# Conditioning visits of a fused decoder layer regrouped from eight to five, and three more of its first projections' phases taken in quarters

## The chip, the cores and the metric

One core of a Trainium2 chip runs the whole kernel. The metric is the device time of one execution in microseconds (us). Times of the profile are counted from the first instruction of the profiled execution.

## The reference, cut to what matters

One layer of a hybrid decoder for 256 prompt tokens and 8 sample tokens (264 columns), D = 2048, all in float32:

```python
mod = silu(c) @ ada_w + ada_b                      # 9 conditioning vectors
shift, scale, gate = split(mod, 3)
h = rmsnorm(x, g_pre) * (1 + scale) + shift
z = h @ w_in                                       # a_x, a_g, q, k, v, b_g
y_a = pool_mixer(a_x) * silu(a_g)
y_b = groupnorm(retention(q, k, v)) * silu(b_g)
ya, yb = y_a @ w_a_proj, y_b @ w_b_proj
g_a, g_b = split(sigmoid(h @ w_merge + b_merge), 2)
out = rmsnorm((g_a * ya + g_b * yb) @ w_out, g_post)
y = x + gate * out
```

## The kernel before, in words

The kernel is written engine by engine, each with its own program and with semaphores between them; the order in each program is the order of the work. All transfers are issued by SyncE, one after the other. Weights come in units of 1 MB (128 partitions by 2048 numbers, `UNIT`). A product in float32 is made of three passes of the faster format: ScalarE copies a unit to its high part (`w_hi`, `split`, L792), VectorE subtracts it from the raw unit (`w_lo`, L1132), and TensorE multiplies high by high, high by low and low by high (`sum_up`, L442 to L444), 48 matmuls of 264 columns for a unit, one project of some 5.8 us.

**The first phases (L589 to L611).** h can't be made before the conditioning is known, so the kernel goes over K in eight phases p, each for two of the 16 tiles of h. Phase p needs four units of conditioning weights (`ada_phase`, 64 small matmuls, L416), a selection (`select`, L435), the making of two tiles of h on VectorE and ScalarE (`make_h`, `split_h`, `low_h`), and then the products of slices 2p and 2p+1 (`first_w`): each slice holds, for these two tiles of K, eight of the 16 first gate projections. Five of the 16 sums stay in banks of PSUM (`own`); eleven pass through two banks in turn (`pass_through`) and are added up in SBUF by VectorE (`take_sum`, L1165), so that TensorE waits for VectorE two sums later. Slices 0 to 6 are handled in quarters (`BY_QUARTER`, L70): VectorE reports every quarter of the low part, TensorE takes two of the eight units of a slice per quarter (`quarter`, L529), and an even slice begins with a special order (`first_quarter`, L545). In this form (p = 1 to 3) TensorE's conditioning for phase p stands behind the first quarter of slice 2p-1, and VectorE takes sums of slice 2p-1 ahead of the pieces of slice 2p. From p = 4 on (L605) a slice is waited for as a whole, the conditioning stands ahead of slice 2p-1 (`odd_slice`, `even_slice`), and VectorE splits all four pieces of slice 2p ahead of the first sum of slice 2p-1 (L1268 to L1270). The first slice is loaded by one transfer (`load_slice(0)`, L283).

**The middle.** Stream units 0 to 71: eight heads of retention, four groups of pooling, eight units for ya.

**The last stretch.** Projects q = 0 to 31 (`project(12, q, ...)`, L715) are units 72 to 103: for q = 0 to 7 only yb's projections, since their 16 gates came out of the first phases; they were stored to DRAM and are read back in pairs (`sig_a`, `sig_b`, `load_gates`, L371). `combine(n)` on VectorE (L1482) makes gate times ya plus gate times yb; it needs the output of project n, which ScalarE takes from its bank (L1027). The gates' buffers are single, so the load of pair n waits for combine(n - 1), `mf_ready`. Between projects TensorE makes the gate's part of the conditioning: 16 units (`ada1`), two at each of eight visits behind projects 3, 7, 11, 14, 18, 22, 26 and 29 (`COND_VISITS`, L76, L720), 16 small matmuls a unit as the trace counts them (`gate_unit`, L426), out of a ring of two (`gate_ring`). Their loads stand in SyncE's passes q of this loop:

```python
for i in range(75, 107):
    q = i - 75
    load(12, i - 72)
    if q < FIRST // 2 - 1:
        load_gates(q + 1)
    for s in range(2):
        if q - 1 - s in COND_VISITS[:7]:
            load_cond(COND_VISITS.index(q - 1 - s) + 1, s)
```

`load` waits until VectorE has split the unit that used the slot before (`lo_ready`), `load_gates(q + 1)` for combine(q), `load_cond` until TensorE has used the slot. SyncE stands still at each such wait.

Of the kernel before, what the change touches and what calls it, by code (L numbers as in the profile page):

```python
# [69 lines left out]
BY_QUARTER, HIGH_BY_QUARTER = (0, 1, 2, 3, 4, 5, 6), (0, 1, 2, 4, 6)  # L70
# [5 lines left out]
COND_VISITS = (3, 7, 11, 14, 18, 22, 26, 29)  # L76
# [20 lines left out]
def build(nc, stream, first_w, ada0, ada1, xT, x_tok, consts_in, headc, trig, cnt_in, poolw, spool,  # L97
# [5 lines left out]
    with ctx:  # L103
        def sb(name, shape, dt=f32, stack=ctx):
            return stack.enter_context(nc.sbuf_tensor(name, shape, dt))
# [66 lines left out]
        late = ExitStack()  # L172
        m_hi = sb("m_hi", [128, KT, NT], f32r, late)
        ya_out = sb("ya_out", [128, KT, NT], f32, late)
        m_lo = sb("m_lo", [128, KT, NT], f32r, late)
# [30 lines left out]
        ada_half = sem("ada_half")  # L206
# [29 lines left out]
        gate_loaded = [sem(f"gate_loaded{s}") for s in range(2)]  # L236
# [14 lines left out]
        Y_BANK = [TR, TV, SC, O1, ST, P[0], P[1], TR]  # L251

# [4 lines left out]
        def _(sp):  # L257
# [25 lines left out]
            load_slice(0)  # L283
            for p in range(1, 4):
                load_slice(2 * p - 1)
                load_ada(p, range(4))
                load_slice(2 * p)
            for p in range(4, 8):
                load_ada(p, (0, 1))
                load_slice(2 * p - 1)  # L290
                load_ada(p, (2, 3))
                load_slice(2 * p)
# [84 lines left out]
            def load_cond(v, s):  # L377
                if v >= 1:
                    sp.wait_ge(gate_used, 2 * v - 1 + s)
                sp.dma_start(gate_ring[:, s, :], ada1[2 * v + s]).then_inc(gate_loaded[s], 16)  # L380
# [3 lines left out]
            load_cond(0, 0)  # L384
            load_cond(0, 1)
            for i in range(75, 107):
                q = i - 75
                load(12, i - 72)
                if q < FIRST // 2 - 1:
                    load_gates(q + 1)  # L390
                for s in range(2):
                    if q - 1 - s in COND_VISITS[:7]:
                        load_cond(COND_VISITS.index(q - 1 - s) + 1, s)
# [15 lines left out]
        def _(pe):  # L409
# [183 lines left out]
            for p in range(1, 4):  # L593
# [8 lines left out]
            first_quarter(6)  # L602
            for n in range(1, 4):
                quarter(6, n)
            for p in range(4, 8):  # L605
                ada_phase(p)
                odd_slice(2 * p - 1, between=p)
                if p < 7:
                    even_slice(2 * p)
# [105 lines left out]
            for q in range(32):  # L715
# [4 lines left out]
                if q in COND_VISITS:  # L720
                    v = COND_VISITS.index(q)
                    if v == 4:
                        pe.wait_ge(gpart_ready, 1)
                    for s in range(2):
                        pe.wait_ge(gate_loaded[s], 16 * v + 16)
                        gate_unit(2 * (v % 4) + s, gate_ring[:, s, :]).then_inc(gate_used, 1)
# [54 lines left out]
        def _(act):  # L781
# [74 lines left out]
            for p in range(1, 4):  # L856
# [6 lines left out]
            for p in range(4, 8):  # L863
                split_slice(2 * p)
                ada_copy(p)
                split_h(p)
                split_slice(2 * p + 1)
# [250 lines left out]
        def _(dve):  # L1118
# [115 lines left out]
            for p in range(1, 4):  # L1234
# [23 lines left out]
            for p in range(4, 8):  # L1258
# [419 lines left out]
```

## Time and profile before

| | before |
|---|---|
| median of 3 runs | 929.7 us (929.62 to 929.83) |
| the profiled execution | 929.46 us |
| its span, first to last instruction | 927.6 us |
| TensorE busy | 911.0 us, 98% |
| VectorE busy | 554.2 us, 60% |
| ScalarE busy | 420.3 us, 45% |
| DMA | 234.58 MB, mean 253 GB/s |
| mean granted TensorE clock | 0.997 |
| chain that ended last, by engine | PE 93%, DMA 4%, DVE 1% |

PE is TensorE, PEld its weight loads, DVE VectorE, ACT ScalarE, SP or SPq SyncE, L a line of the kernel. Matmuls overlap: one is listed with 0.28 us, but the next starts 0.12 us after it, so the distances of starts are to be read. An idle time in brackets stands before the instruction of its row, with what ended it. Granted clock is the share of full speed: 1.00 is 2.4 GHz, 0.50 is 1.2 GHz.

### The profile page before, as it was taken

The page shows a single profiled execution, that of the slowest core. Times are in us where ns is not written, and L with a number is a line of the kernel's source. Part 1 is how long each engine was busy: PE and PEld are TensorE (multiplying, and loading weights), DVE is VectorE, ACT ScalarE, POOL GpSimd, SP SyncE. Part 2 cuts the span into 40 slices and gives each one's busy share as a digit, 9 for nine tenths or more (in the row PEclk, how much of TensorE's full clock was granted, in tenths as well). Part 3 has the DMA queues.
Part 4 walks back from the last instruction along what each step waited for, and adds up shares of the span by engine and source line. Part 5 has one row for each costly group of instructions (what it writes and reads, how often), then busy time and mean ns, then how long its engine had stood idle before and what let it go on. Part 6 is the DMA issues. An engine that isn't in the chain of part 4 may idle for free.

```text
span 927.6 us, 18788 instructions
## 1 busy us (share of the span) xinstructions
PE 911.0 (98%) x7816; PEld 873.8 (94%) x7816; DVE 554.2 (60%) x809; ACT 420.3 (45%) x537; POOL 54.9 (6%) x38
## 2 busy tenths in 40 slices
PE   6999999999999999999999999999999999999997
PEld 4888889999999999999999999999999999999997
DVE  4667776467575766757576655336454434446664
ACT  3424237556465665646454433444343434343330
POOL 0000000001102020120202122000000000000000
PEclk9999999999999999999999999999999999999999
DMA  9999985848576584857675555466787676744535
GB/s 365 420 420 418 419 330 198 323 145 318 182 292 231 206 301 152 323 188 275 243 274 177 194 203 188 152 272 189 279 309 289 243 259 241 258 156 177 182 137 187
DMA packets 43467, 234.58 MB, mean 253 GB/s; under 512 B 8848, under 2 KB 14224, under 8 KB 16656
## 3 DMA queue, kind: packets, MB, share of 16 engines
q1 hardware_dynamic: 43408, 233.72, 68.2%
q8 instruction: 46, 0.75, 0.3%
q14 instruction: 13, 0.11, 0.0%
HBM read 219.33 MB, written 14.38 MB: 252 GB/s over the span
## 4 chain that ended last, share of the span: by engine, by line
PE 93%; DMA 4%; DVE 1%; SPq 1%; POOL 1%; issue 0%; ACT 0%; DVEq 0%; POOLq 0%
PE bank L442 25%; PE bank L443 25%; PE bank L444 25%; DMA raw<-first_w 4%; PE bank L507 3%; PE bank L508 3%; PE bank L509 3%; PE bank L416 2%; PE bank L426 2%; PE bank L657 1%; PE bank L702 1%; PE bank L641 1%; DVE raw L1564 1%; PE bank L552 1%; PE bank L642 0%; PE bank L666 0%
## 5 line engine op out<-in xcount | busy, mean ns | idle before, releaser
L442 PE MATMUL bank<-h_hi,w_hi 128*128 128x264 f32 x1280 | 368.2, 288 | 0.0
L443 PE MATMUL bank<-h_lo,w_hi 128*128 128x264 f32 x1280 | 362.8, 283 | 0.0
L444 PE MATMUL bank<-h_hi,w_lo 128*128 128x264 f32 x1280 | 362.5, 283 | 0.0
L1132 DVE TENSOR_TENSOR w_lo<-raw,w_hi 128x2048 fp32r<-128x2048 f32 x119 | 272.3, 2288 | 141.2 <-PE bank L444 139.4
L792 ACT ACTIVATE w_hi<-raw 128x2048 fp32r<-128x2048 f32 x120 | 229.8, 1915 | 40.9 <-DMA raw<-stream 20.9
L442 PEld LDWEIGHTS bank<-h_hi,w_hi 128*128 128x128 f32 x1280 | 241.1, 188 | 6.1 <-issue 5.8
L443 PEld LDWEIGHTS bank<-h_lo,w_hi 128*128 128x128 f32 x1280 | 241.3, 189 | 0.3
L444 PEld LDWEIGHTS bank<-h_hi,w_lo 128*128 128x128 f32 x1280 | 240.1, 188 | 0.0
L442 PE MATMUL bank<-yb_hi,w_hi 128*128 128x264 f32 x256 | 72.8, 284 | 0.0
L507 PE MATMUL bank<-h_hi,w_hi 128*128 128x264 f32 x240 | 71.7, 299 | 1.1 <-DVE gate_sum L1165 0.9
L442 PE MATMUL bank<-m_hi,w_hi 128*128 128x264 f32 x256 | 72.7, 284 | 0.0
L444 PE MATMUL bank<-yb_hi,w_lo 128*128 128x264 f32 x256 | 72.6, 283 | 0.0
L443 PE MATMUL bank<-m_lo,w_hi 128*128 128x264 f32 x256 | 72.5, 283 | 0.0
L444 PE MATMUL bank<-m_hi,w_lo 128*128 128x264 f32 x256 | 72.5, 283 | 0.0
L443 PE MATMUL bank<-yb_lo,w_hi 128*128 128x264 f32 x256 | 72.5, 283 | 0.0
L509 PE MATMUL bank<-h_hi,w_lo 128*128 128x264 f32 x240 | 68.2, 284 | 0.0
L508 PE MATMUL bank<-h_lo,w_hi 128*128 128x264 f32 x240 | 68.2, 284 | 0.0
L507 PEld LDWEIGHTS bank<-h_hi,w_hi 128*128 128x128 f32 x240 | 45.2, 188 | 5.5 <-issue 3.8
L442 PEld LDWEIGHTS bank<-yb_hi,w_hi 128*128 128x128 f32 x256 | 48.2, 188 | 0.8 <-issue 0.8
L1079 POOL TENSOR_TENSOR sq_t<-o_t 128x528 f32<-128x528 f32 x8 | 23.5, 2940 | 425.3 <-DVE o_t L1351 425.3
L443 PEld LDWEIGHTS bank<-m_lo,w_hi 128*128 128x128 f32 x256 | 48.2, 188 | 0.0
L443 PEld LDWEIGHTS bank<-yb_lo,w_hi 128*128 128x128 f32 x256 | 48.2, 188 | 0.0
(189 smaller groups left out, 1205.9 us busy)
## 6 DMA issues: line engine op xcount, KB each, us to landing
raw<-stream SPq DMA_DIRECT2D x120, 1024.0 KB, 5.0
ada_ring<-ada SPq DMA_DIRECT2D x31, 1024.0 KB, 19.4
raw<-first_w SPq DMA_DIRECT2D x16, 1024.0 KB, 16.0
gate_ring<-ada SPq DMA_DIRECT2D x16, 1024.0 KB, 6.9
s_t<-sret SPq DMA_DIRECT2D x8, 1024.0 KB, 5.0
v_all<-v_dram SPq DMA_DIRECT2D x8, 1024.0 KB, 6.7
nret_s<-s_t SPq DMA_DIRECT2D x8, 1024.0 KB, 7.8
x_t<-xT SPq DMA_DIRECT2D x4, 528.0 KB, 6.0
```

The costliest lines, as they stand in the source:

```text
L416: mm = pe.matmul(TR[32 * j:32 * j + 32, 0:AW], cpad[:, 8 * (j % 2) + 2 * s + kk, :], w[:, at:at + AW], start=(s == 0 and kk == 0), stop=(s ...
L426: mm = pe.matmul(TR[32 * j:32 * j + 32, 0:AW], cpad[:, 2 * v + kk, :], w[:, at:at + AW], start=(v == 0 and kk == 0), stop=(v == 7 and kk = ...
L442: pe.matmul(out, wh[:, cols], hi[:, k, :], start=(k == 0), stop=False)
L443: pe.matmul(out, wh[:, cols], lo[:, k, :], start=False, stop=False)
L444: mm = pe.matmul(out, wl[:, cols], hi[:, k, :], start=False, stop=(k == depth - 1))
L507: pe.matmul(out, hi, h_hi[:, k, :], start=(start and t == 0), stop=False)
L508: pe.matmul(out, hi, h_lo[:, k, :], start=False, stop=False)
L509: mm = pe.matmul(out, lo, h_hi[:, k, :], start=False, stop=(stop and t == 1))
L552: pe.matmul(FIRST_BANK[u][:, 0:NT], w[:, w_slot, at:at + 128], h[:, 2 * p + t, :], start=start, stop=False)
L792: act.activation(w_hi[:, c % 3, :], raw[:, c % 3, :], ACT.Copy).then_inc(hi_ready, 1)
L1079: pool.tensor_tensor(sq_t[:, :, :], o_t[:, :, :], o_t[:, :, :], ALU.mult).then_inc(sq_ready, 1)
L1132: dve.tensor_tensor(lo, raw[:, c % 3, :], hi.bitcast(f32), ALU.subtract).then_inc(lo_ready, 1)
```

## The change

Three things, with no matmul and no byte more or less.

- The first slice is loaded in two halves, each with a semaphore of its own; ScalarE waits for the first half ahead of its first quarter and for the second ahead of its third.
- Phases 4 to 6 take the form of phases 1 to 3. `BY_QUARTER` goes up to slice 12, the loops over p on all engines now run `range(1, 7)` in quarters, and only phase 7 keeps the form of before. SyncE asks for slice 2p-1 ahead of all four conditioning units of phase p, not behind the first two.
- The gate's 16 units are used at five visits, behind projects 3, 7, 18, 23 and 28, four, four, three, three and two at a time. Three places of a unit each are added to the ring of two, on memory that is not in use yet (`cond_lo` and `cond_hi` on the second halves of `m_lo` and `m_hi`, `cond_ya` on `ya_out`), and a table says in which pass which unit is loaded.

```diff
-BY_QUARTER, HIGH_BY_QUARTER = (0, 1, 2, 3, 4, 5, 6), (0, 1, 2, 4, 6)
+BY_QUARTER, HIGH_BY_QUARTER = tuple(range(13)), (0, 1, 2, 4, 6, 8, 10, 12)
-COND_VISITS = (3, 7, 11, 14, 18, 22, 26, 29)
+COND_VISITS = {3: (0, 1, 2, 3), 7: (4, 5, 6, 7), 18: (8, 9, 10), 23: (11, 12, 13), 28: (14, 15)}
+COND_PLACE = (0, 1, 2, 3, 0, 1, 2, 3, 0, 1, 4, 0, 1, 4, 0, 1)
+COND_LOADS = {0: 1, 1: 2, 3: 3, 4: 4, 5: 5, 6: 6, 7: 7, 11: 8, 12: 9, 13: 10, 19: 11, 20: 12, 21: 13, 24: 14, 25: 15}
...
+        COND = [gate_ring[:, 0, :], gate_ring[:, 1, :], cond_lo[:, :], cond_hi[:, :], cond_ya[:, :]]
...
-            load_slice(0)
-            for p in range(1, 4):
+            for n in range(2):
+                half = slice(UNIT // 2 * n, UNIT // 2 * n + UNIT // 2)
+                sp.dma_start(raw[:, 2, half], first_w[0][:, half]).then_inc((slice_half, raw_loaded[2])[n], 16)
+            for p in range(1, 7):
                 load_slice(2 * p - 1)
                 load_ada(p, range(4))
                 load_slice(2 * p)
-            for p in range(4, 8):
+            for p in range(7, 8):
...
-            def load_cond(v, s):
-                if v >= 1:
-                    sp.wait_ge(gate_used, 2 * v - 1 + s)
-                sp.dma_start(gate_ring[:, s, :], ada1[2 * v + s]).then_inc(gate_loaded[s], 16)
+            def load_cond(u):
+                place = COND_PLACE[u]
+                if u == 3:
+                    sp.wait_ge(proj_done, 80)
+                elif u == 10:
+                    sp.wait_ge(mf_ready, FIRST // 2)
+                elif place in COND_PLACE[:u]:
+                    last = max(n for n in range(u) if COND_PLACE[n] == place)
+                    sp.wait_ge(gate_used, last + 1)
+                sp.dma_start(COND[place], ada1[u]).then_inc(gate_loaded[place], 16)
...
                 if q < FIRST // 2 - 1:
                     load_gates(q + 1)
-                for s in range(2):
-                    if q - 1 - s in COND_VISITS[:7]:
-                        load_cond(COND_VISITS.index(q - 1 - s) + 1, s)
+                if q in COND_LOADS:
+                    load_cond(COND_LOADS[q])
...
                 if q in COND_VISITS:
-                    v = COND_VISITS.index(q)
-                    if v == 4:
-                        pe.wait_ge(gpart_ready, 1)
-                    for s in range(2):
-                        pe.wait_ge(gate_loaded[s], 16 * v + 16)
-                        gate_unit(2 * (v % 4) + s, gate_ring[:, s, :]).then_inc(gate_used, 1)
+                    for u in COND_VISITS[q]:
+                        if u == 8:
+                            pe.wait_ge(gpart_ready, 1)
+                        pe.wait_ge(gate_loaded[COND_PLACE[u]], 16 * COND_PLACE[:u].count(COND_PLACE[u]) + 16)
+                        gate_unit(u % 8, COND[COND_PLACE[u]]).then_inc(gate_used, 1)
...
             def split_quarter(j, n):
-                if n == 0:
+                if j == 0 and n == 0:
+                    act.wait_ge(slice_half, 16)
+                elif n == 0 or (j == 0 and n == 2):
                     act.wait_ge(raw_loaded[slot], 16 * (j // 3) + 16)
```

**SyncE, passes q = 2 to 4 of the last stretch, and the first row of the next.** raw is a project's weights, sig_a and sig_b are a pair of gates, gate_ring and cond_hi places of conditioning units. Before:

```order
L261 DMA raw<-stream 128x2048 [waits lo_ready]
L374 DMA sig_a<-gates_dram 128x264 [waits mf_ready]
L375 DMA sig_b<-gates_dram 128x264
L261 DMA raw<-stream 128x2048 [waits lo_ready]
L374 DMA sig_a<-gates_dram 128x264 [waits mf_ready]
L375 DMA sig_b<-gates_dram 128x264
L261 DMA raw<-stream 128x2048 [waits lo_ready]
L374 DMA sig_a<-gates_dram 128x264 [waits mf_ready]
L375 DMA sig_b<-gates_dram 128x264
L380 DMA gate_ring<-ada 128x2048 [waits gate_used]
L261 DMA raw<-stream 128x2048 [waits lo_ready]
```

After:

```order
L276 DMA raw<-stream 128x2048 [waits lo_ready]
L391 DMA sig_a<-gates_dram 128x264 [waits mf_ready]
L392 DMA sig_b<-gates_dram 128x264
L276 DMA raw<-stream 128x2048 [waits lo_ready]
L391 DMA sig_a<-gates_dram 128x264 [waits mf_ready]
L392 DMA sig_b<-gates_dram 128x264
L403 DMA cond_hi<-ada 128x2048 [waits proj_done]
L276 DMA raw<-stream 128x2048 [waits lo_ready]
L391 DMA sig_a<-gates_dram 128x264 [waits mf_ready]
L392 DMA sig_b<-gates_dram 128x264
L403 DMA gate_ring<-ada 128x2048 [waits gate_used]
```

A conditioning load has come into pass 3: unit 3, into cond_hi, behind that pass's pair. Before, passes 2 and 3 had none, and the load of pass 4 was unit 2; it is unit 4 now.

**TensorE, the first visit.** Before:

```order
L444 MATMUL bank<-yb_hi,w_lo 128x264
L426 MATMUL bank<-gate_ring,cpad 32x256 [waits gate_loaded0]
L426 MATMUL bank<-gate_ring,cpad 32x256 x7
L426 MATMUL bank<-gate_ring,cpad 32x256 [waits gate_loaded1]
L426 MATMUL bank<-gate_ring,cpad 32x256 x7
L442 MATMUL bank<-yb_hi,w_hi 128x264 [waits taken,lo_ready]
L443 MATMUL bank<-yb_lo,w_hi 128x264
```

After:

```order
L465 MATMUL bank<-yb_hi,w_lo 128x264
L447 MATMUL bank<-gate_ring,cpad 32x256 [waits gate_loaded0]
L447 MATMUL bank<-gate_ring,cpad 32x256 x7
L447 MATMUL bank<-gate_ring,cpad 32x256 [waits gate_loaded1]
L447 MATMUL bank<-gate_ring,cpad 32x256 x7
L447 MATMUL bank<-cond_lo,cpad 32x256 [waits gate_loaded2]
L447 MATMUL bank<-cond_lo,cpad 32x256 x7
L447 MATMUL bank<-cond_hi,cpad 32x256 [waits gate_loaded3]
L447 MATMUL bank<-cond_hi,cpad 32x256 x7
L463 MATMUL bank<-yb_hi,w_hi 128x264 [waits taken,lo_ready]
```

Where two units stood there are now four, and the third and fourth wait for loads of their own.

**VectorE, phase 4.** gate_sum rows are sums, w_lo rows pieces of a slice, mods and v_t the making of h. Before:

```order
L1191 SCALAR_TENSOR_TENSOR x_t<-x_t,consts,rstd 128x264 x2
L1149 TENSOR_TENSOR w_lo<-raw,w_hi 128x512 [waits slice_sums,hi_ready]
L1149 TENSOR_TENSOR w_lo<-raw,w_hi 128x512 x3
L1165 TENSOR_TENSOR gate_sum<-bank,gate_sum 128x264 [waits sums_taken,slice_sums]
L1203 TENSOR_TENSOR mods<-bank,consts 128x36 [waits hf_ready,sel_done]
L1213 TENSOR_TENSOR v_t<-x_t,mods 128x2x8 [waits h_lo_ready,h_hi_ready,xn_ready,mod_ready]
L1210 TENSOR_SCALAR v_t<-x_t,mods 128x256
L1216 TENSOR_TENSOR v_t<-v_t,mods 128x2x8 [waits hf_ready]
L1210 TENSOR_SCALAR v_t<-x_t,mods 128x256
L1165 TENSOR_TENSOR gate_sum<-bank,gate_sum 128x264 [waits sums_taken,slice_sums] x2
```

After:

```order
L1209 SCALAR_TENSOR_TENSOR x_t<-x_t,consts,rstd 128x264 x2
L1183 TENSOR_TENSOR gate_sum<-bank,gate_sum 128x264 [waits sums_taken,slice_sums] x2
L1221 TENSOR_TENSOR mods<-bank,consts 128x36 [waits hf_ready,sel_done]
L1231 TENSOR_TENSOR v_t<-x_t,mods 128x2x8 [waits h_lo_ready,h_hi_ready,xn_ready,mod_ready]
L1228 TENSOR_SCALAR v_t<-x_t,mods 128x256
L1234 TENSOR_TENSOR v_t<-v_t,mods 128x2x8 [waits hf_ready]
L1228 TENSOR_SCALAR v_t<-x_t,mods 128x256
L1183 TENSOR_TENSOR gate_sum<-bank,gate_sum 128x264 [waits sums_taken,slice_sums]
L1167 TENSOR_TENSOR w_lo<-raw,w_hi 128x512 [waits slice_sums,hi_quarter]
L1183 TENSOR_TENSOR gate_sum<-bank,gate_sum 128x264 [waits sums_taken,slice_sums]
```

Before, four pieces of slice 8 stood ahead of the first sum of slice 7 and of `mods`; now two sums and `mods` come first, and one piece follows.

## Rows read from the trace of the kernel before

**Rows 1.** The page: busy time and share of each engine; bytes moved in 40 slices.

```profile
PE 911.0 (98%) x7816; PEld 873.8 (94%) x7816; DVE 554.2 (60%) x809; ACT 420.3 (45%) x537; POOL 54.9 (6%) x38
...
GB/s 365 420 420 418 419 330 198 323 145 318 182 292 231 206 301 152 323 188 275 243 274 177 194 203 188 152 272 189 279 309 289 243 259 241 258 156 177 182 137 187
```

**Rows 2.** Chain that ended last, 6 to 34 us: start us, us, what.

```profile
6.54 16.78 DMA raw<-first_w
23.34 0.63 ACT w_hi L807
...
24.42 1.72 PE bank L552 x12
```

**Rows 3.** Timeline of the weight loads, 32 to 38 us: start us, us, instruction [idle before].

```profile
35.64 0.59 PEld L416 LDWEIGHTS bank<-ada_ring,cpad 128*32 128x32 f32 x16 [0.40 <-DMA ada_ring<-ada]
```

**Rows 4.** Timeline of TensorE: where a phase's conditioning begins, seen in short windows.

```profile
49.56 0.42 PE L416 MATMUL bank<-ada_ring,cpad 128*32 128x256 f32 x4
...
66.15 0.63 PE L416 MATMUL bank<-ada_ring,cpad 128*32 128x256 f32 x7
...
80.78 0.42 PE L416 MATMUL bank<-ada_ring,cpad 128*32 128x256 f32 x4
...
97.98 0.42 PE L416 MATMUL bank<-ada_ring,cpad 128*32 128x256 f32 x4
...
114.01 0.64 PE L416 MATMUL bank<-ada_ring,cpad 128*32 128x256 f32 x8
```

**Rows 5.** Chain, 60 to 90 us; then TensorE's timeline at 88.

```profile
64.88 1.29 DVE w_lo L1149 x2
66.19 17.12 DMA raw<-first_w
83.33 1.92 ACT w_hi L799
...
88.17 0.40 PE L507 MATMUL bank<-h_hi,w_hi 128*128 128x264 f32 x1 [0.90 <-DVE gate_sum L1165]
```

**Rows 6.** Timeline of TensorE around a phase's conditioning and around the first two visits.

```profile
65.93 0.29 PE L509 MATMUL bank<-h_hi,w_lo 128*128 128x264 f32 x1
...
69.74 0.39 PE L507 MATMUL bank<-h_hi,w_hi 128*128 128x264 f32 x1
...
644.24 0.28 PE L444 MATMUL bank<-yb_hi,w_lo 128*128 128x264 f32 x1
...
646.32 0.39 PE L442 MATMUL bank<-yb_hi,w_hi 128*128 128x264 f32 x1
646.55 0.28 PE L443 MATMUL bank<-yb_lo,w_hi 128*128 128x264 f32 x1
...
669.72 1.93 PE L426 MATMUL bank<-gate_ring,cpad 128*32 128x256 f32 x32
```

**Rows 7.** Timeline of SyncE's queue: requests behind project 3 and project 6.

```profile
646.38 0.32 SPq L374 DMA_DIRECT2D sig_a<-gates_dram  x1
...
647.22 0.43 SPq L261 DMA_DIRECT2D raw<-stream  x1
...
667.49 0.33 SPq L374 DMA_DIRECT2D sig_a<-gates_dram  x1
...
670.86 0.33 SPq L380 DMA_DIRECT2D gate_ring<-ada  x1
```

**Rows 8.** Issues from 647.2 and from 670.8 us: KB each, us to landing.

```profile
raw<-stream SPq DMA_DIRECT2D x1, 1024.0 KB, 5.0
...
gate_ring<-ada SPq DMA_DIRECT2D x1, 1024.0 KB, 10.4
```

**Rows 9.** Stretches: busy us (x) of PE, PEld, DVE, ACT, POOL; PEclk, DMA share, GB/s.

```profile
9.00:12.00 3.00, 0.00 (x0) 0.00 (x0) 2.86 (x8) 2.51 (x4) 0.00 (x0) 1.00 1.01 426
...
13.00:17.00 4.00, 3.70 (x31) 1.30 (x20) 1.82 (x2) 0.78 (x2) 0.00 (x0) 0.57 1.00 413
...
22.00:25.00 3.00, 1.28 (x12) 1.12 (x11) 1.90 (x6) 1.66 (x4) 0.00 (x0) 1.00 1.02 423
```

More of the change, by code:

```diff
@@ L172, in build @@
         late = ExitStack()
+        with ExitStack() as far:
+            sb("under_hi", [128, KT // 2, NT], f32, far)
+            cond_hi = sb("cond_hi", [128, UNIT], f32, far)
         m_hi = sb("m_hi", [128, KT, NT], f32r, late)
+        with ExitStack() as near:
+            cond_ya = sb("cond_ya", [128, UNIT], f32, near)
         ya_out = sb("ya_out", [128, KT, NT], f32, late)
+        with ExitStack() as far:
+            sb("under_lo", [128, KT // 2, NT], f32, far)
+            cond_lo = sb("cond_lo", [128, UNIT], f32, far)
         m_lo = sb("m_lo", [128, KT, NT], f32r, late)
@@ L205, in build @@
         ada_loaded = [sem(f"ada_loaded{s}") for s in range(8)]
-        ada_half = sem("ada_half")
+        ada_half, slice_half = sem("ada_half"), sem("slice_half")
         ada_used, part_ready, sel_done = sem("ada_used"), sem("part_ready"), sem("sel_done")
@@ L234, in build @@
             sem("yaf_ready"), sem("yahi_ready"), sem("yalo_ready"), sem("npool_ready"), sem("ppool_ready"), sem("ppool_out"))
-        gate_loaded = [sem(f"gate_loaded{s}") for s in range(2)]
+        gate_loaded = [sem(f"gate_loaded{s}") for s in range(5)]
         gate_used, gpart_ready, gsel_done, gbias_ready, gate_ready = (
@@ L375, in load_gates @@
                 sp.dma_start(sig_b[:, :], gates_dram[:, 2 * n + 1, :]).then_inc(gates_in, 16)
-            def load_cond(v, s):
-                if v >= 1:
-                    sp.wait_ge(gate_used, 2 * v - 1 + s)
-                sp.dma_start(gate_ring[:, s, :], ada1[2 * v + s]).then_inc(gate_loaded[s], 16)
+            def load_cond(u):
[8 more added lines that the diff above has]
+                sp.dma_start(COND[place], ada1[u]).then_inc(gate_loaded[place], 16)
             sp.wait_ge(gates_out, 16)
             load_gates(0)
-            load_cond(0, 0)
-            load_cond(0, 1)
+            load_cond(0)
             for i in range(75, 107):
@@ L592, in _ @@
             keep_busy(4)
-            for p in range(1, 4):
+            for p in range(1, 7):
                 first_quarter(2 * p - 2)
@@ L601, in _ @@
                 quarter(2 * p - 1, 3)
-            first_quarter(6)
+            first_quarter(12)
             for n in range(1, 4):
[L604 to L609, printed above, removed]
+                quarter(12, n)
+            ada_phase(7)
+            odd_slice(13, between=7)
             even_slice(14)
@@ L855, in _ @@
                 split_quarter(1, n)
-            for p in range(1, 4):
+            for p in range(1, 7):
                 ada_copy(p)
@@ L862, in _ @@
                 split_slice(2 * p + 1)
[L863 to L867, printed above, removed]
+            split_slice(14)
+            ada_copy(7)
+            split_h(7)
+            split_slice(15)
             split(0, 0)
@@ L1233, in _ @@
             take_sum(0, 4)
-            for p in range(1, 4):
+            for p in range(1, 7):
                 if p >= 2:
@@ L1257, in _ @@
                     split_slice(2 * p, n)
-            for p in range(4, 8):
+            for p in range(7, 8):
                 for b in range(3):
```

## Prediction

> **What bounds the kernel now.** I read the page's shares first: TensorE is busy for 911.0 us, 98% of the span of 927.6 [rows 1], so only what TensorE waits for, or does more or less of, can move the end. The profiled execution took 929.46 us in all, 0.24 below the median of the runs, 929.7; the sum below is made against 929.46 (927.6 of span and 1.9 around it). Then I went through TensorE's timeline for steps between two matmuls that are longer than the usual 0.12 us. Between 24.4 and 917 us there is one real hole, 1.2 us before the matmul at 88.17 [rows 5]; all else sits in the first 24 us or is a tenth or two at a change of operand. So a microsecond of new waiting anywhere in the middle is a microsecond of time.
>
> Four stretches matter for the change.
>
> The start: the chain stands on the transfer of the first slice from 6.54 to 23.3, then ScalarE's split of its first quarter, and TensorE begins at 24.42 [rows 2]. The first conditioning phase after it waits for its last block of weights: the weight load at 35.64 stood idle for 0.40 us until a DMA landed [rows 3].
>
> The first projections: a phase lasts from one row of group 4 to the next. 49.56 to 66.15 is a phase in quarters, 16.59 us; 97.98 to 114.01 is one in whole slices, 16.03 [rows 4].
>
> The hole at 88: the chain goes from the issue of slice 8 at 66.19 to its landing at 83.3, ScalarE's split, and VectorE, which comes to the sum that TensorE waits for only behind four pieces of slice 8 [rows 5].
>
> The gate's conditioning: a visit of two units separates the matmuls at 644.24 and 646.32 [rows 6], and SyncE issues its loads between the gates' loads and the weights' [rows 7], with the times to landing in group 8.
>
> **The first slice in two loads: 0.1 us gained.** ScalarE starts on the first quarter at 23.34 [rows 2]. Half a slice less to land is worth 1.2 us at the 420 GB/s of the page [rows 1], so TensorE could begin near 23.2 at the earliest. But it then comes earlier to the phase at 32.9, whose last block of weights lands at 35.6 whatever TensorE does, since the DMA engines move their 420 GB/s there without a pause and the change sends them no byte less. Today the weight load waits 0.40 [rows 3]; most of that passes beside matmuls of the block before, and I put what TensorE itself gains at 0.1. The Trainium skill (Perfetto Trace Analysis, DMA Optimizations) says that splitting a DMA may let some work start sooner, if the DMA engines are generally idle; here they are not, and the rule's gain of 1.2 us, if it all came through, would make the forecast 1.1 lower.
>
> **Phases 4 to 6 in quarters: 0.5 lost.** VectorE no longer stands at slice 8 with a sum behind it, so the hole at 88 goes: the phase from 80.78 to 97.98 took 17.20 against 16.03 for the next [rows 4], 1.17 gained. The cost is the form itself. In a phase in quarters VectorE's pieces of the odd slice come between the sums, and TensorE waits a little for each: VectorE's two pieces from 64.88 on, which the chain passes through just ahead of slice 8's request, are such a place [rows 5]. All of them make 16.59 - 16.03 = 0.56 per phase. Three phases turn into this form: 1.68 lost. In all 1.68 - 1.17 = 0.5 lost. Slices 7, 9 and 11 are requested ahead of their phase's conditioning weights and land earlier, slices 8, 10 and 12 and the last weights of each phase land when they do now (same bytes ahead of them), and TensorE comes to them later by its half microsecond; no new wait there. Bounds: 0.6 gained (if the later phases, further behind their data, show a third of the 0.56) and 0.7 lost.
>
> **Five visits for eight: 1.0 gained.** Four units lie between the matmuls at 65.93 and 69.74, 3.81 us; two between 644.24 and 646.32, 2.08 [rows 6]. Two units are 1.73, so going there and back costs 2.08 - 0.12 - 1.73 = 0.23, and the first matmul after it takes 0.11 longer (646.32 to 646.55 for 0.12). 0.34 for each visit, three fewer: 1.0. Matmuls and bytes stay as they are.
>
> **Unit 3 comes too late: 5.3 lost.** The first visit now wants units 0 to 3 behind project 3. Unit 3's load stands in SyncE's pass q = 3 behind that pass's pair of gate loads, and the pair waits for combine(3), which needs project 3's own output. In the trace of before that pair goes out at 646.38, and the next request at 647.22 [rows 7] lands 5.0 us later [rows 8], at 652.2. That next request is unit 3 after the change. TensorE leaves project 3 at 644.4 and needs 0.2 and three units (2.6) until it asks for unit 3, at 647.1. It stands from there to 652.2: 5.1 us, with nothing of its own to do, since the queue is strictly in order and project 4, whose weights are split, stands behind unit 3. Behind it nothing else is late: ScalarE and VectorE catch up in this time. Units 1 and 2 now also travel in passes 0 and 1, ahead of weights that ScalarE waits for, which can make combine(3) up to 1.2 later. Bounds 5.0 and 6.3; I take 5.3, near the row. The Trainium skill (DMA: Bandwidth & Descriptors, Anatomy of one DMA) gives 2.0 us and the bytes at 436 GB/s for a DMA of the GpSimd path, 4.4 us for this megabyte; as an estimate by that page the wait would be 0.6 shorter, but the trace has 5.0 for the same transfer and that is used.
>
> **Unit 7 comes later still: 8.0 lost.** The second visit wants units 4 to 7 behind project 7. Units 4 and 5 take places where the before loads units 2 and 3, and are in time. Unit 6 goes out behind the pair that waits for combine(6), unit 7 one pass later behind another megabyte of weights. In the before's own times the pair goes out from 667.49 on, and the third megabyte behind it, issued at 670.86 [rows 7], takes 10.4 us [rows 8], so lands at 681.3; unit 7 will be that third megabyte. The visit behind project 7 begins at 669.72 [rows 6], three units later it is 672.3: 8.9 us of wait. If all is as quick as around 647, it is less: project 6 ends 5.8 (48 matmuls) before 669.6, the pair goes out 1.9 later as there, the next request 0.85 after it, the first megabyte lands in 5.0 and each behind it in 2.5 (its time at 420 GB/s). Unit 7 lands at 676.6, a wait of 4.3. I take 8.0, near the row of the same place. The wait has two parts, with unit 6 between them. Visits 18, 23 and 28 load two or more passes ahead: no wait, as in the eight visits now.
>
> **The clock: 3.4 lost.** The one long pause of the trace: TensorE did nothing from 9 to 12, and in the stretch from 13 to 17 the granted clock is 0.57 [rows 9], that is 3.4 us at 1.2 GHz and the rest at 2.4. Everything that runs at the lower level takes twice as long, so 3.4 us of it lose 1.7. Two pauses, both longer than that one, make 3.4 in all. Bounds: 0 (no fall) and 5 (half as long again at each).
>
> **Sum.** 929.46 - 0.1 + 0.5 - 1.0 + 5.3 + 8.0 + 3.4 = 945.6. Against the median this is about 16 us, 1.7%, slower. What a measurement of this kernel tells from no change is about 0.2%, 1.9 us.
>
> **Rivals.**
>
> (a) The waits come, the clock stays at the upper level: 945.6 - 3.4 = 942.2. For it: TensorE works only 1.28 us of the stretch from 22 to 25, and the clock stays at 1.00 [rows 9]. Against: that pause is shorter than the one from 9 to 12.
>
> (b) The wait for unit 7 is the short one, 4.3, because during the pause for unit 3 the other engines and the queue catch up and never fall behind again: 945.6 - 3.7 = 941.9, and with no fall of the clock 938.5. Against: between the two visits four projects pass with their loads, as in the before.
>
> (c) Faster: the loads are out in time. It would take a SyncE that does not hold unit 3 for combine(3), so that the request leaves by 647.1 - 5.0 = 642.1; likewise unit 7 by 667. Then only the gains are left: 929.46 + 0.4 - 1.0 = 928.9, and with the whole 1.2 of the first slice and no loss by the quarters, 926.1. Against it stands the order of the requests and the rows at 646.38: the pair can't leave before project 3 is done.
>
> (d) The change's aim is met in part: only unit 3 is late, and short, and the time stays within 0.2%. This needs waits of under 2.5 us in all, and the shorter of the two bounds above, 4.3, is more than that alone.
>
> **Chances.** Forecast 0.55; (a) 0.20; (b) 0.18; (c) 0.04; (d) 0.03. The range reaches from the low end of (b) without a clock fall, 938.5, with half a microsecond for the good bounds of the other terms, so 938.0, to all bounds at the bad end: 929.46 + 0.7 - 1.0 + 6.3 + 8.9 + 5 = 949.4, so 949.5. Faster 0.04, within 0.2% 0.03, slower 0.93.
>
> **What would show it.** In the profile after: TensorE idle before a conditioning matmul near 647 by about 5 us, ended by a DMA into cond_hi, and again near 675 to 680 by about 8 in two parts, ended by DMAs into cond_lo and cond_hi; PEclk below 9 in the slices around them. The phases' first conditioning matmuls stand 16.6 apart, the hole at 88 is gone, the seventh phase begins near 130.5 instead of 130.07. TensorE begins near 23.2 but still leaves the first phase near 36.6. If no DMA into cond_hi ends a wait, the forecast is wrong at its root; if the waits are there but the clock stays at 1.00, (a) holds; if the phases stand 16.0 apart, the quarter's price was wrong.

## The result, and the profile after

The changed kernel takes 949.2 us (median of 5 runs, 947.0 to 950.5) where the kernel before takes 929.6: a ratio of 1.0204, 95% interval 1.0193 to 1.0216. It is slower by 2.0%. The forecast was 945.6, the range 938.0 to 949.5: the side is right, the size 3.6 us short. The profiled execution took 950.09 us, its span is 948.3.

The page of the kernel after, against [rows 1] (TensorE, and its granted clock in 40 slices):

```profile
PE 918.4 (97%) x7816; PEld 878.5 (93%) x7816; DVE 552.1 (58%) x809; ACT 419.9 (44%) x546; POOL 54.9 (6%) x38
...
PEclk8999999999999999999999999997979999999999
```

TensorE has the same 7816 matmuls and is busy for 7.4 us more, in a span that is 20.7 us longer. So it stands more, and it does the same work more slowly, in the two slices (23.7 us each) where PEclk shows 7. TensorE's timeline there names both, against [rows 6] (start us, us, instruction, in brackets the idle time before it and what ended it):

```profile
645.32 1.93 PE L447 MATMUL bank<-gate_ring,cpad 128*32 128x256 f32 x32
647.07 1.05 PE L447 MATMUL bank<-cond_lo,cpad 128*32 128x256 f32 x16
657.75 1.93 PE L447 MATMUL bank<-cond_hi,cpad 128*32 128x256 f32 x16 [9.64 <-DMA cond_hi<-ada]
659.61 0.59 PE L463 MATMUL bank<-yb_hi,w_hi 128*128 128x264 f32 x1
...
661.03 0.29 PE L463 MATMUL bank<-yb_hi,w_hi 128*128 128x264 f32 x1
...
683.60 1.93 PE L447 MATMUL bank<-gate_ring,cpad 128*32 128x256 f32 x32
688.81 1.94 PE L447 MATMUL bank<-cond_lo,cpad 128*32 128x256 f32 x16 [3.28 <-DMA cond_lo<-ada]
693.79 1.93 PE L447 MATMUL bank<-cond_hi,cpad 128*32 128x256 f32 x16 [3.04 <-DMA cond_hi<-ada]
695.65 0.59 PE L463 MATMUL bank<-h_hi,w_hi 128*128 128x264 f32 x1
...
698.46 0.29 PE L463 MATMUL bank<-h_hi,w_hi 128*128 128x264 f32 x1
```

The places are those forecast, units 3, 6 and 7. The first wait is not 5.1 but nearly 10 us. Behind each wait a unit of conditioning takes 1.86 us from its first matmul to the next instruction (657.75 to 659.61), and the first project matmul behind it reads 0.59 where it reads 0.39 in [rows 6] (646.32); from 661.03 on they read 0.29 again. The granted clock in stretches (busy us of PE, PEld, DVE, ACT, POOL; PEclk, DMA share, GB/s):

```profile
651.00:658.00 7.00, 0.25 (x4) 0.20 (x8) 3.24 (x4) 2.22 (x2) 0.00 (x0) 0.50 0.76 266
...
692.00:698.00 6.00, 4.21 (x26) 2.94 (x27) 0.00 (x0) 2.47 (x2) 0.00 (x0) 0.50 0.77 287
```

0.50 is the lower of the two levels, 1.2 GHz. It lasted from about 650.7 to 661.0 and from 688.2 to 698.5 (the microseconds 650:651, 661:662, 688:689 and 698:699 read 0.84, 1.00, 0.61 and 0.77). Of the first stretch some 7 us fall into the standing itself, of the second 3.7; the rest is work. Why the first wait is so long is read from the chain that ended last, 636 to 654 us:

```profile
636.95 10.68 DMA raw<-stream
...
647.77 1.70 issue
649.47 0.41 ACT m_hi L1036
...
651.29 0.45 DVE m_f L1505
...
651.76 0.32 SPq L391
...
652.60 5.11 DMA cond_hi<-ada
```

Unit 3's own transfer takes 5.1 us, as forecast (5.0 [rows 8]). But its request goes out at 652.60, because the pair of pass 3 leaves at 651.76, 5.4 later than in [rows 7] (646.38). Of these, 0.9 is this execution's later start (its first `yb_hi` matmul stands at 622.02, at 621.16 before), 4.5 is new. The chain shows what held it: not TensorE's project 3, which ended at 645.3, but the weights 77 (stream unit 77, `raw<-stream`, asked for in pass 2), which took 10.68 us to land. ScalarE's timeline shows the same from its side, first of the kernel before, then of the one after:

```profile
640.98 1.92 ACT L792 ACTIVATE w_hi<-raw 128x2048 fp32r<-128x2048 f32 x1 [1.76 <-DMA raw<-stream]
...
644.62 0.39 ACT L1027 ACTIVATE yb_out<-bank 128x264 f32<-128x264 f32 x1 [1.42 <-PE bank L444]
```

```profile
638.93 1.92 ACT L809 ACTIVATE w_hi<-raw 128x2048 fp32r<-128x2048 f32 x1 [4.66 <-DMA raw<-stream]
...
647.66 1.91 ACT L809 ACTIVATE w_hi<-raw 128x2048 fp32r<-128x2048 f32 x1 [6.22 <-DMA raw<-stream]
649.47 0.41 ACT L1036 ACTIVATE m_hi<-m_f 128x264 fp32r<-128x264 f32 x1
649.79 0.37 ACT L1045 ACTIVATE yb_out<-bank 128x264 f32<-128x264 f32 x1
```

ScalarE takes project 3's sum (`yb_out`) only behind the split of these weights. Before, the split was done early and ScalarE waited 1.42 us for the sum; now the weights land 6.7 us later (647.63 for 640.95), and the sum waits for them. In these passes SyncE asks for unit 1 right ahead of the weights 76, then for unit 2 right ahead of the weights 77:

```profile
630.62 0.43 SPq L403 DMA_DIRECT2D gate_ring<-ada  x1
631.10 0.43 SPq L276 DMA_DIRECT2D raw<-stream  x1
...
636.48 0.43 SPq L403 DMA_DIRECT2D cond_lo<-ada  x1
636.95 0.43 SPq L276 DMA_DIRECT2D raw<-stream  x1
```

The first conditioning matmuls of the first phases, against [rows 4], stand 16.5 apart as long as they are in quarters (the two between stand at 99.76 and 116.24), and 14.7 at the end of them:

```profile
66.73 0.64 PE L437 MATMUL bank<-ada_ring,cpad 128*32 128x256 f32 x8
...
83.25 0.42 PE L437 MATMUL bank<-ada_ring,cpad 128*32 128x256 f32 x4
...
130.94 0.42 PE L437 MATMUL bank<-ada_ring,cpad 128*32 128x256 f32 x4
```

From 66.73 to 130.94 are 64.21 us, against 63.92 before (66.15 to 130.07): 0.3 lost. The hole at 88 of [rows 5] is gone.

### The profile page after: what moved, and what is told of

Same layout as the page of the kernel before. It is cut to its first block, busy times and chain, and to the rows that moved or that the text cites. A ratio compares the mean times of both kernels' runs of the same rounds, so it can differ in the third digit from the quotient of the medians.

```text
span 948.3 us, 18810 instructions
## 1 busy us (share of the span) xinstructions
PE 918.4 (97%) x7816; PEld 878.5 (93%) x7816; DVE 552.1 (58%) x809; ACT 419.9 (44%) x546; POOL 54.9 (6%) x38
## 4 chain that ended last, share of the span: by engine, by line
PE 91%; DMA 5%; DVE 1%; SPq 1%; issue 1%; POOL 1%; ACT 0%; DVEq 0%; ACTq 0%; POOLq 0%
PE bank L463 24%; PE bank L464 23%; PE bank L465 23%; PE bank L528 4%; PE bank L437 3%; PE bank L529 3%; PE bank L530 3%; DMA raw<-stream 2%; DMA cond_hi<-ada 2%; PE bank L447 1%; PE bank L573 1%; DMA ada_ring<-ada 1%; PE bank L675 1%; PE bank L720 1%; PE bank L659 1%
## 5 line engine op out<-in xcount | busy, mean ns | idle before, releaser
L463 PEld LDWEIGHTS bank<-h_hi,w_hi 128*128 128x128 f32 x1280 | 242.1, 189 | 5.2 <-issue 4.5
L465 PEld LDWEIGHTS bank<-yb_hi,w_lo 128*128 128x128 f32 x256 | 48.4, 189 | 0.0
L463 PEld LDWEIGHTS bank<-m_hi,w_hi 128*128 128x128 f32 x256 | 48.3, 189 | 0.0
```

Source lines behind the costliest of these rows:

```text
L463: pe.matmul(out, wh[:, cols], hi[:, k, :], start=(k == 0), stop=False)
L465: mm = pe.matmul(out, wl[:, cols], hi[:, k, :], start=False, stop=(k == depth - 1))
```

## The experiments

Theory at the outset: the waits for units 3, 6 and 7 and the clock that falls in them make all of the loss; the first wait is long because units 1 and 2 crowd the projects' weights. Rivals: the new form of the phases costs more than 0.5; the waits are a matter of the crossing megabytes and not of when a request leaves. Intervals are 95%. The executions of the changed kernel itself spread over 3.5 us (947.0 to 950.5), so differences of a microsecond between the runs below are read from traces, not from medians: from the first `yb_hi` to the first `m_hi` matmul, the first matmuls of the two last stretches of projections, it is 202.59 us before and 222.52 in the changed kernel.

**Phases and first slice alone** (e1_stage). The changed kernel with the eight visits of before.

```diff
-COND_VISITS = {3: (0, 1, 2, 3), 7: (4, 5, 6, 7), 18: (8, 9, 10), 23: (11, 12, 13), 28: (14, 15)}
+COND_VISITS = (3, 7, 11, 14, 18, 22, 26, 29)
...
-                if q in COND_LOADS:
-                    load_cond(COND_LOADS[q])
+                for s in range(2):
+                    if q - 1 - s in COND_VISITS[:7]:
+                        load_cond(COND_VISITS.index(q - 1 - s) + 1, s)
```

> The change without its third part: first slice in two loads, phases 4 to 6 in quarters, conditioning visits as before. My theory (the phases in quarters cost 0.5 each and win back 1.17 once, and the first slice's gain is taken away by the conditioning weights that land at 35.6): 0.2 to 0.5 us slower than before, 929.9, the eighth phase beginning 0.3 to 0.5 later than before. Rival (the start's gain of 1.2 us comes through): 928.7 or less. If this part held any of the 20 us, it would show here as 932 or more.

Measured: 929.85 us against 929.63, ratio 1.0002 (0.9993 to 1.0011). So the other 19.3 us are all the visits'; from `yb_hi` to `m_hi` it is 202.58, as before. Its phases run from 66.59 to 130.81, 64.22 us, as in the changed kernel.

**The units' requests ahead of the gates' pair** (e2_ahead).

```diff
-                if q < FIRST // 2 - 1:
-                    load_gates(q + 1)
                 if q in COND_LOADS:
                     load_cond(COND_LOADS[q])
+                if q < FIRST // 2 - 1:
+                    load_gates(q + 1)
```

> As the change, but in each pass the conditioning unit's load stands ahead of the pair of gates' loads instead of behind it. My theory (unit 3 is held by the pair, which waits for project 3's own output): unit 3 is asked for some 8 us earlier, lands behind its pass's weights at about 653.5 and the first wait falls from 10 us to about 6; unit 6 comes in time, unit 7 one megabyte earlier; in all 939 to 942. Rival (the DMA engines are simply full there, and no order helps): within 2 us of the change, 947 or more.

Measured: 937.7 us, ratio 1.0094 (1.0076 to 1.0111), 11.5 less than the change. The four executions took 936.1, 936.2, 939.1 and 939.9 us with mean granted clocks of 0.997, 0.998, 0.989 and 0.991. The trace is of the first, in which the clock is at the lower level only from 680.2 to 683.6; that it fell for longer in the last two is likely by their means, but no trace shows it. TensorE's timeline:

```profile
649.22 1.07 PE L447 MATMUL bank<-cond_hi,cpad 128*32 128x256 f32 x16 [1.67 <-DMA cond_hi<-ada]
...
675.37 1.05 PE L447 MATMUL bank<-cond_lo,cpad 128*32 128x256 f32 x16
680.44 1.93 PE L447 MATMUL bank<-cond_hi,cpad 128*32 128x256 f32 x16 [4.02 <-DMA cond_hi<-ada]
```

Unit 6 (`cond_lo` at 675.37) comes in time, unit 3 is late by 1.7, unit 7, still asked for in the pass of its own visit, by 4.0. The same bytes in the same stretch: what moved is the moment of the request. The edit moves every conditioning request, though. Units 1 and 2 leave a pass's wait earlier too, right behind weights instead of right ahead of them (unit 2 at 630.53, 0.5 behind the weights 76), and the pair of pass 3 leaves at 646.67. So this run holds two effects, and the runs on units 1 and 2 below say what that part is worth.

**Units 1 and 2 loaded ahead of the loop** (e3_pre12).

```diff
-COND_LOADS = {0: 1, 1: 2, 3: 3, 4: 4, ...
+COND_LOADS = {3: 3, 4: 4, ...
...
             load_cond(0)
+            load_cond(1)
+            load_cond(2)
```

> As the change, but units 1 and 2 are loaded ahead of the loop, beside unit 0, and not in passes 0 and 1. The first wait was 10.0 us, not 5.3. My theory now: 5.1 of it is unit 3's own transfer, the other 5 come from units 1 and 2, which stand ahead of the weights of projects 4 and 5; ScalarE waits for these weights ahead of its copies of yb, so combine(2) and combine(3) and the pair of pass 3 come late. Then the first wait is 5 to 6 us here, the pair of pass 3 goes out near 646.5 to 647.5 as before the change, and the time is about 5 us less than the change's, 944, with the clock's part perhaps less too. Rival (unit 3's transfer is slow by itself, or the combine is late for another reason): first wait 8 us or more, time within 2 us of the change's.

Measured: 946.0 us, ratio 1.0169 (1.0154 to 1.0185). The pair of pass 3 leaves at 646.87, as in the kernel before, and the wait is inside the forecast's bounds for it (5.0 to 6.3):

```profile
653.76 1.93 PE L449 MATMUL bank<-cond_hi,cpad 128*32 128x256 f32 x16 [6.02 <-DMA cond_hi<-ada]
```

So units 1 and 2 are worth 3.6 us of the first wait (9.64 less 6.02), and from `yb_hi` to `m_hi` 3.1 us (219.46). This removed them from the passes altogether, and does not tell whether their bytes or their place ahead of the weights did the harm.

**The same bytes behind the weights** (e5_order).

```diff
-COND_LOADS = {0: 1, 1: 2, 3: 3, 4: 4, ...
+COND_LOADS = {3: 3, 4: 4, ...
...
                 load(12, i - 72)
+                if q in (1, 2):
+                    load_cond(q)
                 if q < FIRST // 2 - 1:
                     load_gates(q + 1)
```

> The changed kernel with one edit in SyncE's program: units 1 and 2 are requested in passes 1 and 2, right behind the pass's weights, where they stood right ahead of the next pass's weights. The same bytes go out in the same stretch, within half a microsecond. Theory of the order (a pass is a ring: weights land, ScalarE splits them, then does its part of the combine, then the gates' pair goes out, then the next weights; a megabyte ahead of the weights lengthens the ring by 2.5 us, one behind them does not): the pair of pass 3 goes out at 646.5 to 647.5 instead of 651.8, the wait for unit 3 is 5.5 to 7 us instead of 10.0, the time 945 to 946.5, as with the two units loaded ahead of the loop. Theory of the bytes (two megabytes more are 5 us more of the DMA engines, wherever they stand): the pair leaves near 651, the wait stays near 10, the time 948.5 to 949.5. The prediction's bound (at most 1.2 for both) would be right for neither.

Measured: 946.6 us, ratio 1.0178 (1.0161 to 1.0195), as with the units out of the way; from `yb_hi` to `m_hi` it is 219.37 us, 3.1 less than in the change. SyncE's queue, and TensorE at unit 3:

```profile
630.07 0.43 SPq L276 DMA_DIRECT2D raw<-stream  x1
630.55 0.43 SPq L403 DMA_DIRECT2D gate_ring<-ada  x1
...
646.80 0.32 SPq L391 DMA_DIRECT2D sig_a<-gates_dram  x1
```

```profile
653.18 1.93 PE L449 MATMUL bank<-cond_hi,cpad 128*32 128x256 f32 x16 [5.62 <-DMA cond_hi<-ada]
```

One place in the queue, half a microsecond in time, moved the pair of pass 3 from 651.8 to 646.8 (0.5 of it is the change's later start). It is the order: a pass is a ring (weights land, ScalarE splits them, takes the sum, VectorE combines, the pair goes out, then the next weights are asked for), and a megabyte ahead of the weights lengthens the ring each time round. The wait for unit 3 is 4.0 us shorter, the stretch only 3.1: behind unit 3 twelve project matmuls now run at the lower clock where there were six (655.04 to 657.85), which takes 0.7 back.

**Idle matmuls in the waits** (e4_busy). TensorE runs matmuls on constants into a bank nobody reads while units 3, 6 and 7 travel.

```diff
                         if u == 8:
                             pe.wait_ge(gpart_ready, 1)
+                        keep_busy({3: 40, 6: 15, 7: 10}.get(u, 0))
```

> As the change, but TensorE does 40 idle matmuls (some 9 us, into a bank that nobody reads then) ahead of its wait for unit 3, 15 ahead of unit 6 and 10 ahead of unit 7, all inside the waits. My theory (the pauses let the clock fall to 1.2 GHz, which costs 1.6 us after the first and 2.3 after the second): granted clock 1.00 throughout the stretch, the waits' ends as before, time 3 to 4.5 us less than the change's, 945 to 946. Rival (the lower clock costs nothing there, the time is the waits alone): the same time as the change.

Measured: 944.9 us, ratio 1.0162 (1.0146 to 1.0177), 4.3 less than the change (from `yb_hi` to `m_hi` 217.52 us, 5.0 less). Its timeline:

```profile
648.96 9.20 PE L502 MATMUL bank<-consts 128*128 128x128 f32 x80
658.09 1.07 PE L447 MATMUL bank<-cond_hi,cpad 128*32 128x256 f32 x16
659.09 0.39 PE L463 MATMUL bank<-yb_hi,w_hi 128*128 128x264 f32 x1
...
684.36 3.62 PE L502 MATMUL bank<-consts 128*128 128x128 f32 x30
687.90 1.07 PE L447 MATMUL bank<-cond_lo,cpad 128*32 128x256 f32 x16
688.91 2.50 PE L502 MATMUL bank<-consts 128*128 128x128 f32 x20
691.82 1.07 PE L447 MATMUL bank<-cond_hi,cpad 128*32 128x256 f32 x16 [0.42 <-DMA cond_hi<-ada]
```

The waits stay, filled; the unit behind them takes 1.00 us (658.09 to 659.09) and not 1.86. In this run the clock stood at 1.00 from 21.8 on until the last microseconds. The three fillings are 9.1, 3.5 and 2.9 us long, 15.6 in all where the change's waits come to 17.0 (worked out below), so of the gain about 1.4 us are shorter waits and not clock, which leaves 3.6 of the 5.0.

**The first slice in two loads, alone** (s1_slice): the change's two loads and its two waits of ScalarE, in the kernel before.

```diff
-            load_slice(0)
+            for n in range(2):
+                half = slice(UNIT // 2 * n, UNIT // 2 * n + UNIT // 2)
+                sp.dma_start(raw[:, 2, half], first_w[0][:, half]).then_inc((slice_half, raw_loaded[2])[n], 16)
```

> The kernel before with one edit: the first slice in two loads. The theory of the prediction (the first phase's last weights land when they do now, so TensorE's earlier start is lost again 10 us later): TensorE begins near 23.2 instead of 24.4, a hole of 1 to 2 us opens before the last block of the first conditioning phase, and the time is 929.5, 0.1 below before. Rival (splitting a transfer lets the work start sooner and it stays sooner): 928.4, 1.2 below, with no hole.

Measured: 930.0 us against 929.95, ratio 0.9996 (0.9987 to 1.0005), so nothing; the rival's 1.2 lies at the very end of the interval, and the trace decides against it. TensorE begins at 23.61 instead of 24.42 (23.91 and 25.13 in two other runs with the one load), and loses it again where forecast, at the last weights of the first phase, against [rows 3]:

```profile
35.97 1.07 PE L418 MATMUL bank<-ada_ring,cpad 128*32 128x256 f32 x16 [1.02 <-DMA ada_ring<-ada]
```

The rule of the Trainium skill (Perfetto Trace Analysis, DMA Optimizations) hangs its promise on DMA engines that are generally idle. The trace agrees with that condition: the stretches 22:25 and 30:34 of this run have a DMA share of 1.01 and 1.02, and the split is worth nothing.

**Phase 4 alone in quarters** (s2_four), phases 5 to 7 in whole slices.

```diff
-BY_QUARTER, HIGH_BY_QUARTER = (0, 1, 2, 3, 4, 5, 6), (0, 1, 2, 4, 6)
+BY_QUARTER, HIGH_BY_QUARTER = (0, 1, 2, 3, 4, 5, 6, 7, 8), (0, 1, 2, 4, 6, 8)
...
-            for p in range(1, 4):
+            for p in range(1, 5):
...
-            for p in range(4, 8):
+            for p in range(5, 8):
```

> The kernel before with one edit: phase 4 alone in quarters, phases 5 to 7 in whole slices. Theory (the hole of 1.17 at 88 goes, one phase pays 0.5 to 0.56 for the form): phases 66.15 to 82.7 and 82.7 to 98.8, the later ones 16.0 apart, and 929.0, 0.6 below before. Rival (the hole only moves one phase on, to the sum that then stands behind slice 10): it shows before a matmul near 104, and the time is 929.6 to 930.1. What is known so far, phases 4 to 6 in quarters with the first slice, 929.85, does not tell these apart.

Measured: 929.8 us against 929.95, ratio 0.9997 (0.9988 to 1.0006). The time alone does not tell 0.6 from nothing. The trace does, for the stretch itself: from 66.40 to 129.64, 63.24 us, 0.68 less than before, and no hole near 104. The same stretch varies by 0.2 where nothing in it was changed (63.70 in s3_visits, whose hole at 88 is shorter), so the sign is shown and the size only to some tenths.

**The five visits placed otherwise** (s3_visits), in the kernel before; the edit is shown against the change's tables and loop.

```diff
-COND_VISITS = {3: (0, 1, 2, 3), 7: (4, 5, 6, 7), ...
-COND_LOADS = {0: 1, 1: 2, 3: 3, 4: 4, 5: 5, 6: 6, 7: 7, 11: 8, ...
+COND_VISITS = {4: (0, 1, 2, 3), 7: (4, 5, 6, 7), ...
+COND_LOADS = {0: (1,), 1: (2,), 3: (3,), 5: (4, 5), 6: (6, 7), 11: (8,), ...
...
+                for u in COND_LOADS.get(q, ()):
+                    load_cond(u)
                 if q < FIRST // 2 - 1:
                     load_gates(q + 1)
-                if q in COND_LOADS:
-                    load_cond(COND_LOADS[q])
```

> The kernel before with the five visits alone, placed and loaded otherwise than in the change: visits behind projects 4, 7, 18, 23 and 28; unit 3 is requested in pass 3, units 4 and 5 in pass 5, units 6 and 7 in pass 6, and in each pass ahead of the gates' pair for the next one. If the waits of the change are a matter of when the requests go out, none of over 0.5 us is left at the gate's conditioning, the clock stays at 1.00 and only the gain of three visits fewer is left: 928.6, 1.0 below before. If the crowding of the early units with weights still makes a wait (two units in one pass, 2.5 us of extra transfer each), one of 1 to 3 us shows before unit 3, 6 or 7, and the time is 930 to 932. If there is no wait and nothing gained, three visits fewer are worth nothing and 929.6 comes out.

Measured: 928.9 us against 929.95, ratio 0.9987 (0.9978 to 0.9996). The first `yb_hi` and the first `m_hi` matmul stand 201.83 apart here (621.54 and 823.37), 202.59 in the kernel before (621.16 and 823.75). One short wait is left, 0.6 us for the weight load of unit 7.

**All three parts, each as it should be by now** (s4_all): the edits of s1_slice, s2_four and s3_visits together.

> The three parts together, as each should be by now: first slice in two loads, phase 4 alone in quarters, five visits behind projects 4, 7, 18, 23, 28 with loads a pass earlier. Additive theory: 929.6 - 0.1 - 0.6 - 1.0 = 927.9. If the kernel has a slack that takes such gains back later (data that comes no earlier), it stays within 0.5 of 929.6. If the visits still wait, 1 to 3 us above 927.9.

Measured: 928.25 us (927.4 to 929.5, 11 runs) against 929.95, ratio 0.9982 (0.9973 to 0.9992). It is 1.7 us faster than the kernel before, 0.7 to 2.5 by the interval, and 21 faster than the change, where 927.9 was expected. From `yb_hi` to `m_hi` it is 201.51 us. SyncE asks for unit 3 at 641.87 and for units 6 and 7 by 663.21, and TensorE runs the four units of the first visit without a pause, in 3.6 us:

```profile
641.87 0.43 SPq L400 DMA_DIRECT2D cond_hi<-ada  x1
...
663.21 0.43 SPq L400 DMA_DIRECT2D cond_hi<-ada  x1
```

```profile
649.90 1.93 PE L444 MATMUL bank<-gate_ring,cpad 128*32 128x256 f32 x32
...
653.49 0.39 PE L460 MATMUL bank<-yb_hi,w_hi 128*128 128x264 f32 x1
```

## Why the prediction was right, and where it was short

| Term | Forecast | Measured | From |
| --- | --- | --- | --- |
| First slice in two loads | -0.1 | 0.0 | s1_slice; hole in the first phase |
| Phases 4 to 6 in quarters | +0.5 | +0.3 | 64.21 against 63.92 |
| Three visits fewer | -1.0 | -0.8 to -1.1 | traces of s3_visits, s4_all |
| Wait for unit 3 | +5.3 | +9.7 | 657.75 less 648.04 |
| Waits for units 6 and 7 | +8.0 | +7.3 | 3.35 and 3.97 |
| Clock | +3.4 | +3.6 | rows at either level |
| Sum, from 929.46 | 945.6 | 949.4 | |

Measured here means: a unit takes 0.97 to 1.00 us and two take 1.86 at the upper clock (rows of e4_busy), and what lies between that and the next matmul of the changed kernel is wait. Unit 2 begun at 647.07 would end at 648.04; units 4 and 5 begun at 683.60 at 685.46; unit 6 begun at 688.81 at 689.82. The clock: unit 3 took 1.86 for 1.00, the 6 matmuls behind it 1.42 (659.61 to 661.03) for 0.84; unit 7 0.86 more, the 12 matmuls behind it 2.81 (695.65 to 698.46) for 1.56. 0.86 + 0.58 + 0.86 + 1.25 = 3.55. The sum comes to 949.4, the median is 949.2. The terms are of the profiled execution, which took 950.09 and began 0.67 later than the one before (25.09 for 24.42); with that the sum is 950.0. The traces give the stretch by itself: from the first `yb_hi` to the first `m_hi` 222.52 us (622.02 to 844.54) against 202.59, so 19.9 more, where the terms say 9.7 + 7.3 + 3.6 - 1.0 = 19.6.

That 949.2 lies inside the range is partly luck: it does so by 0.3 us, and the profiled execution, 950.09, lies outside it. The wait for unit 3 was 9.7, far outside its own bounds of 5.0 and 6.3; the range held because the other terms stayed short of the bad ends that they were given (7.3 for 8.9, 3.6 for 5, 0.3 for 0.7).

**Unit 3** is the step that failed, and in one place. That TensorE stands from 647.1 until unit 3 lands, the strict queue, the transfer of 5.0 us: all as forecast (5.1). What failed is "that pair goes out at 646.38", with the reservation that units 1 and 2 "can make combine(3) up to 1.2 later". It was 4.5 later (5.4 with the later start). I had priced the two megabytes as a small disturbance of a pass with slack. The slack is there, but it is the 1.42 us that ScalarE waits for the sum, and it is spent once, while the two transfers add up: the weights 76 landed 4.1 us later than before (638.91 for 634.84) and the weights 77 6.7 (both with the 0.9 of the start), because unit 2 and the weights 77 queue behind what unit 1 had put back. 5.8 less 1.4 is the 4.4 that the pair is late. By the prediction's own 2.5 us for a megabyte, less the 1.4 of ScalarE's row before, the bound had to be 3.6 us and not 1.2. The remaining microsecond goes with a slower channel, which the stretches of the kernel after show (DMA share and GB/s last):

```profile
637.00:642.00 5.00, 5.00 (x44) 5.00 (x43) 1.48 (x3) 2.50 (x3) 0.00 (x0) 1.00 0.98 372
642.00:647.00 5.00, 5.00 (x61) 4.25 (x63) 3.17 (x4) 0.00 (x0) 0.00 (x0) 1.00 0.89 283
```

The engines are nearly full and move less than 420. What slows them is not shown: the gates' small rows travel among the weights, but they do so in e5_order too, where the first of these stretches has 409 GB/s. e3_pre12 and e5_order show the rest: without the bytes, or with them behind the weights, the pair leaves at 646.9 and 646.8.

**Unit 7** was right in mechanism and near in size, 7.3 for 8.0, partly by luck. The forecast took the pair's lead over the visit from the kernel before, 2.2 us (667.49 to 669.72); rival (b) had it at 4.0, since the queue would have caught up during the first stand. It was 2.9 (680.72 to 683.60): caught up in part, for the weights 80, asked for in pass 5, were 7.2 us on their way (669.44 to 676.60) and ScalarE split them ahead of the sum that the pair waits for. Rival (b) also took 5.0 for the first megabyte behind the pair, but that one, unit 6, needed 7.1 (681.67 to 688.77), with the pass before still in the channel. Unit 7 took 11.1 (682.62 to 693.75), near the 10.4 of [rows 8]. Rival (c)'s condition was too mild in the same way: e2_ahead asked for unit 3 at 642.18, where (c) had 642.1 as early enough, and it held TensorE until 649.2, since behind its pass's weights it needed 7.0 us and not 5.0.

**The clock** came as forecast in size, 3.6 for 3.4, and partly by luck: the forecast gave each pause 3.4 us at the lower level. It lasted about 10 us each time, but began in the waits, and only 3.3 and 4.7 us of the work that TensorE was late for ran in it (units 3 and 7 and the matmuls behind them; what unit 6 lost was hidden in the wait for unit 7). Rival (a) is excluded, by PEclk and by e4_busy. **Three visits fewer** are worth 0.8 to 1.1 for the 1.0 forecast. **The quarters' price**: three phases in the form and the hole gone make +0.30, one phase and the hole gone make -0.68; the difference is two phases, so one costs 0.49 instead of 0.56, and the hole was worth the 1.17 forecast, within the 0.2 by which the hole itself varies.

**The first slice**: right, with a hole before the last weights. "TensorE begins near 23.2" could not be seen in the changed kernel's own profile, where its first loads landed a microsecond late (it began at 25.09); e1_stage began at 23.28 and s1_slice at 23.61.

## What to carry to other kernels

When a transfer is put into a queue that also feeds a ring of producer and consumer, place it behind the ring's own transfer: one place earlier in two turns of the ring here made the ring 4.5 us late and the kernel 3.1 us slower, one place later made neither. In this kernel, with steps of 5.8 us, a load that was wanted behind step q and left behind a request that waits for step q itself came 5.7 to 9.7 us late, behind one that waits for step q - 1 still 1.7 to 4.0 (e2_ahead, and units 6 and 7 of the change), behind one that waits for step q - 2 at most 0.6 (s3_visits, s4_all). With visits and requests moved by both rules the same change, with one phase in quarters instead of three, went from 20 us slower to 1.7 faster. And a long wait of TensorE costs more than itself: 17 us of waiting took 3.6 more at the lower clock.

## What the runs showed of the hardware that I had not expected

A much shorter pause than those of the change can be followed by the lower clock, and is not always. In the kernel before TensorE stood for 1.2 us ahead of 88.17 and the granted clock stayed at 1.00, as it did behind the 1.7 us ahead of 649.22 in e2_ahead. In s1_slice the pause at the same place was 1.45 us (87.56 to 89.02), and the stretches around it read:

```profile
87.00:89.00 2.00, 0.85 (x7) 0.63 (x6) 2.00 (x5) 0.00 (x0) 0.00 (x0) 1.00 1.00 414
89.00:93.00 4.00, 3.98 (x20) 3.98 (x21) 2.40 (x9) 2.10 (x3) 0.00 (x0) 0.58 1.01 416
```

The phase around it took 19.23 us (81.11 to 100.34) against 17.20, and that execution 931.78 us against a median of 930.0. Whether some slower executions of the kernel before have the same cause is only a guess: its profile does not show it. That same pause is removed by s2_four and s4_all, so it may be worth more than its 1.2 us in the executions in which this happens.

The transfer of one megabyte took 5.1 us with little else under way (`cond_hi` at 652.60) and 11.1 as the third of its pass. The Trainium skill (DMA: Bandwidth & Descriptors, Anatomy of one DMA) gives, for a DMA of the GpSimd path, 2.0 us and the bytes at 436 GB/s, as an estimate 4.4 us for this one. The trace has 0.7 more for SyncE's transfer even when it is nearly undisturbed, and the measurement decides.
